# Normalisation ahead of the rotation in a softmax pipeline, and an interleaved tail behind the last experts

## The chip, the cores and the metric

The kernel runs on one core of a Trainium2 chip. The metric is the device time in microseconds of one execution, as the median of several runs. All matrices and activations are float32. Where a matmul must be accurate, the kernel splits an operand into a high part (`_hi`, type fp32r) and the rest (`_lo`), and adds the products; a full f32 matmul is used for the smaller products and appears in the trace as two records.

## What is computed

The kernel computes a two-layer block (retention, RWKV, gated units, FFN; untouched here), and then a second block with dilated attention, memory cross-attention and a mixture of experts, closed by a root-mean-square norm. Cut to what the change touches:

```python
def rms_norm(t, g):
    tf = t.astype(jnp.float32)
    y = tf * lax.rsqrt(jnp.mean(tf * tf, axis=-1, keepdims=True) + NORM_EPS)
    return (y * g.astype(jnp.float32)).astype(t.dtype)

# dilated attention, 12 heads of 64 channels, 512 tokens
qf, kf = rotary_2(q, positions), rotary_2(k, positions)
s = einsum(qf, kf) * HEAD_DIM ** -0.5        # masked
m = jnp.max(s, axis=-1)
p = jnp.exp(s - m[..., None]); den = jnp.sum(p, axis=-1)
o = einsum(p, v) / den

# second block, its end
h = rms_norm(x, moe_norm_g)
x = x + hierarchical_moe(h, ...)             # 32 experts, top 2 of a group
return rms_norm(x, final_norm_g)
```

## The kernel before

Activations lie transposed in SBUF: `xT` is 128 partitions by 8 tiles by 512 tokens. Each engine has its own instruction list, written out by hand in the order in which it runs; engines meet at semaphores only (`wait_ge`, `then_inc`). There is no scheduler, so the order in the source is the order of execution.

**The middle stage** (`mid_phase`) is a row of 62 jobs `n`, each one weight tile times activations on TensorE, into PSUM bank `n % 2`. For each job ScalarE makes the high part of the weights (`high`, a cast) and GpSimd the low part (`low`, a subtraction of two SBUF tiles, 128x1024), one or two jobs ahead. Between the jobs lies the attention. It handles the heads in six pairs `g`, each spread over four steps that go with jobs `n = 8 + 4g` to `11 + 4g` (`att_step(n)` gives `g, step`). Its parts are:

- `turn` (TensorE) and `half_turn`, `times_cos`, `finish_turn` (VectorE, GpSimd, VectorE): the rotation of q and k. It follows one job behind the jobs listed in `TURNED` (4, 5, 8, 9, 10, 11, 14 to 17, 20, 21). `half_turn` frees the rotation's PSUM bank, and `finish_turn` needs the product by GpSimd.
- `scores(g, s)` (TensorE), `mask_scores(g, s)` (VectorE: adds the band and takes the row maximum), `exps(g, s)` (ScalarE), all with `s` = the step, in steps 0 and 1. `s` says which half of the query tiles.
- `normalise(g, s)` (VectorE): a reciprocal of the sums and four divisions of 128x512, in step `s + 1`. It waits for the exponentials of half `s`.
- `swing(g, u)` (TensorE): 16 transposes of the probabilities of head `u`, in steps 2 and 3. In step 2 it waits for six divisions of the pair, that is, for two of the four in `normalise(g, 1)`. `take_swung` copies the result out of PSUM on VectorE and ScalarE; `values` multiplies by v.
- `tap`: the depthwise convolution, four multiply-adds per step on VectorE until job 20. `take_mem_k` (jobs 22 to 29) and `put` (pairs 3 to 5) are further work of VectorE in the same steps.

**The expert stage** (`experts_phase`) handles 32 experts, two at a time (`g` = 0 to 15), in quads. Per two experts TensorE multiplies up (L3098), turns the result (L3122) and multiplies down in two halves of 512 columns (`y_banks`, L3133). ScalarE writes `y_hi` and VectorE `y_lo` of each half (L3210, L3278). `scatter(g, k)` (L3110, L3111) brings tile `k` of the result back to the tokens, in one of the two `add_banks`, and `add` (L3231) adds the bank to `xT`. For all but the last two experts the scatters lie between the matmuls of the next up product.

**The end.** Behind the last experts' block the flag `again` is loaded (L3315) to see whether an expert had more than 64 tokens; the body under the `If` holds further rounds. Then `norm_phase` squares the eight tiles on ScalarE (L180), sums them over the partitions on TensorE by a matmul with ones (L194), takes the root by Ln and Exp (L134, L136) and scales on VectorE into `hT` (L206). A last block sends `hT` out as one DMA (L3358) and waits for it. Between two blocks all engines meet.

## Time and profile before

| | |
|---|---|
| median of 3 runs | 3269.89 us (3269.32 to 3277.79) |
| the profiled execution | 3263.98 us, of it span 3262.1 us |
| granted TensorE clock, mean | 0.963 of full |
| TensorE matmul busy | 2996.3 us, 92% |
| VectorE busy | 1239.5 us, 38% |
| ScalarE busy | 1039.2 us, 32% |
| GpSimd busy | 1056.6 us, 32% |

The attention stretch of the middle stage lies at 2250 to 2480 us, the expert stage at 2750 to 3233 us. Everything is told against the span of the one profiled execution; the median of the runs is 5.9 us above that execution's own time. In a timeline, a row merges instructions of a kind that follow each other; the bracket at its end is the idle time of that engine just before, and what ended it. Where a row of matmuls is longer than its like, the granted clock was lower. PEld is TensorE's weight load, SPq the queue of the engine that issues DMAs.

### The profile page before, as it was taken

To read this page: it belongs to the slowest core of one execution; us is meant where nothing else is said; L and a number is where in the kernel's file an instruction comes from. 1 tells how busy PE (TensorE), PEld (TensorE's weight loads), DVE (VectorE), ACT (ScalarE), POOL (GpSimd) and SP (SyncE) were. 2 spreads that over 40 slices of the span, in tenths; PEclk is the share of its full clock that TensorE was granted. 3 is DMA by queue.
4 is the path that set the end of the run, shared out by engine and by line. 5 is a ranking of instruction groups with operands and counts; after the bars stand their busy time and mean duration, and the time that the engine had idled before them with its cause. 6 is when DMAs were issued, how large, how long until landed. Compare 5 with 4: busy or idle time off the path is not lost. (4 is left out here: it accounts for less than half of the span.)

```text
span 3262.1 us, 48752 instructions
## 1 busy us (share of the span) xinstructions
PE 2996.3 (92%) x20676; PEld 2256.8 (69%) x20677; DVE 1239.5 (38%) x1762; ACT 1039.2 (32%) x1525; POOL 1056.6 (32%) x635
## 2 busy tenths in 40 slices
PE   5997989989999699798999999989888998999997
PEld 4776878878888577597887888857666764444542
DVE  2248424334440124842333444037764323222222
ACT  3443233333332235322423333235345331111111
POOL 2343224434444233422443444423334330011000
PEclk8998999999999899899999999989999999999998
DMA  3220022212222222001222222221112236999994
GB/s 129 69 72 26 4 82 91 90 66 95 99 105 89 89 78 71 31 4 63 97 91 79 79 102 100 89 93 52 52 54 93 66 141 261 374 401 401 399 378 181
DMA packets 52911, 402.71 MB, mean 123 GB/s; under 512 B 7008, under 2 KB 8160, under 8 KB 12512
## 3 DMA queue, kind: packets, MB, share of 16 engines
q1 hardware_dynamic: 52704, 399.72, 32.2%
q8 instruction: 157, 2.57, 0.3%
q14 instruction: 50, 0.41, 0.0%
HBM read 397.60 MB, written 2.10 MB: 123 GB/s over the span
## 5 line engine op out<-in xcount | busy, mean ns | idle before, releaser
L1138 POOL TENSOR_TENSOR back_w_lo<-w,back_w_hi 128x1024 fp32r<-128x1024 f32 (+1 forms) x248 | 537.4, 2177 | 751.1 <-ACT back_w_hi L1347 751.0
L1347 ACT CAST back_w_hi<-w 128x1024 fp32r<-128x1024 f32 (+1 forms) x248 | 236.8, 955 | 809.9 <-PE bank L1166 773.6
L1161 PE MATMUL bank<-h_hi,back_w_hi 128*128 128x512 f32 x1056 | 265.9, 394 | 11.1 <-ACT back_w_hi L1347 11.1
L1163 PE MATMUL bank<-h_lo,back_w_hi 128*128 128x512 f32 x1056 | 260.8, 389 | 0.0
L1166 PE MATMUL bank<-h_hi,back_w_lo 128*128 128x512 f32 x1056 | 260.8, 389 | 0.0
L322 POOL TENSOR_TENSOR front_w_lo<-w,front_w_hi 128x1024 fp32r<-128x1024 f32 x68 | 167.6, 2467 | 245.8 <-ACT front_w_hi L499 245.8
L1161 PEld LDWEIGHTS bank<-h_hi,back_w_hi 128*128 128x128 f32 x1056 | 200.1, 190 | 56.4 <-ACT back_w_hi L1347 13.1
L3098 PE MATMUL bank<-moe_w,moe_hg 128*64 128x512 f32 x1024 | 232.5, 597 | 0.0
L1897 POOL TENSOR_TENSOR mid_w_lo<-w,mid_w_hi 128x1024 fp32r<-128x1024 f32 x62 | 150.4, 2427 | 246.9 <-ACT mid_w_hi L2357 246.6
L1163 PEld LDWEIGHTS bank<-h_lo,back_w_hi 128*128 128x128 f32 x1056 | 198.3, 188 | 41.3
L1166 PEld LDWEIGHTS bank<-h_hi,back_w_lo 128*128 128x128 f32 x1056 | 198.2, 188 | 41.1
L3098 PEld LDWEIGHTS bank<-moe_w,moe_hg 128*64 128x64 f32 x1024 | 71.0, 137 | 134.9 <-issue 134.9
L1544 DVE SCALAR_TENSOR_TENSOR back_conv<-bank,back_taps,back_conv 128x511 f32<-128x511 f32 x88 | 66.0, 750 | 255.2 <-ACT back_conv L1448 255.2
L377 PE MATMUL bank<-h_hi,front_w_hi 128*128 128x512 f32 x416 | 119.9, 433 | 44.9 <-ACT front_w_hi L499 44.9
L499 ACT CAST front_w_hi<-w 128x1024 fp32r<-128x1024 f32 x68 | 70.9, 1046 | 255.9 <-PE bank L382 200.9
L3231 DVE TENSOR_TENSOR xT<-xT,bank 128x512 f32<-128x512 f32 x128 | 82.3, 683 | 170.2 <-PE bank L3111 170.2
L1511 DVE TENSOR_TENSOR xT<-xT,bank 128x512 f32<-128x512 f32 (+1 forms) x36 | 22.6, 628 | 307.0 <-PE bank L1166 305.2
L377 PEld LDWEIGHTS bank<-h_hi,front_w_hi 128*128 128x128 f32 x416 | 80.6, 199 | 77.4 <-issue 60.5
L3133 PE MATMUL bank<-moe_w,moe_midT 128*64 128x512 f32 x512 | 113.4, 595 | 12.1 <-ACT moe_midT L3205 12.1
L382 PE MATMUL bank<-h_hi,front_w_lo 128*128 128x512 f32 x416 | 109.0, 405 | 12.4 <-POOL front_w_lo L322 12.4
L3039 POOL COPY moe_quad_place<-moe_place 128x16 f32 (+1 forms) x7 | 1.4, 198 | 365.7 <-PE bank L3117 365.7
L2357 ACT CAST mid_w_hi<-w 128x1024 fp32r<-128x1024 f32 x62 | 64.8, 1045 | 159.4 <-PE bank L1976 97.3
(544 smaller groups left out, 5690.6 us busy)
## 6 DMA issues: line engine op xcount, KB each, us to landing
moe_w<-in_moe_w SPq DMA_DIRECT2D x128, 1024.0 KB, 11.5
moe_w<-in_moe_w SPq DMA_DIRECT2D x32, 2048.0 KB, 11.7
w<-in_ffn_up SPq DMA_DIRECT2D x44, 1024.0 KB, 4.8
w<-in_w_merge SPq DMA_DIRECT2D x24, 1536.0 KB, 6.4
w<-in_w_in SPq DMA_DIRECT2D x34, 1024.0 KB, 4.8
w<-in_w_mid SPq DMA_DIRECT2D x31, 1024.0 KB, 4.8
w<-in_ffn_down SPq DMA_DIRECT2D x16, 1408.0 KB, 6.0
w<-in_w_out SPq DMA_DIRECT2D x16, 512.0 KB, 4.1
```

The costliest lines, as they stand in the source:

```text
L322: nc.gpsimd.tensor_tensor(split(w_lo, c, t), raw(c, t), split(w_hi, c, t).bitcast(F32), ALU.subtract).then_inc(f["w_lo"], 1)
L377: nc.tensor.matmul(T.ps[t][:, :], w_hi[:, t, k, :], h_hi[:, k, :], start=(k == 0), stop=False)
L382: mm = nc.tensor.matmul(T.ps[t][:, :], w_lo[:, t, k, :], h_hi[:, k, :], start=False, stop=(k == KD - 1))
L1138: nc.gpsimd.tensor_tensor(split(B.w_lo, n), raw(n), split(B.w_hi, n).bitcast(F32), ALU.subtract).then_inc(f["w_lo"], 1)
L1161: nc.tensor.matmul(bank, B.w_hi[:, n % 2, k, :], x_hi[:, cols], start=start and k == 0, stop=False)
L1163: nc.tensor.matmul(bank, B.w_hi[:, n % 2, k, :], x_lo[:, cols], start=False, stop=False)
L1166: mm = nc.tensor.matmul(bank, B.w_lo[:, n % 2, k, :], x_hi[:, cols], start=False, stop=stop and k == len(hi) - 1)
L1347: nc.scalar.copy(split(B.w_hi, n), raw(n)).then_inc(f["w_hi"], 1)
L1897: nc.gpsimd.tensor_tensor(split(B.w_lo, n), raw(n), split(B.w_hi, n).bitcast(F32), ALU.subtract).then_inc(f["w_lo"], 1)
L3098: mm = nc.tensor.matmul(bank[half_of(u), :], hg[:, k, slots_of(b, u)], w[:, u, k * 512:k * 512 + 512], start=(k == 0), stop=(k == KD - 1))
L3133: mm = nc.tensor.matmul(y_banks[half][half_of(u), :], midT[:, f, half_of(u)], w2[:, u, c:c + 512], start=(f == 0), stop=(f == 3))
L3231: nc.vector.tensor_tensor(T.xT[:, k, :], T.xT[:, k, :], add_banks[k % 2][:, :], ALU.add).then_inc(sems["added"], 1)
```

## The change

1. In `mid_phase`, VectorE's `normalise` moves ahead of `half_turn`, `mask_scores` and `finish_turn` of the same step. 
2. For the last two experts the scatters use six PSUM banks in turn (6, 7, 4, 5, 0, 1) instead of two. The first four start when `y_lo`'s first half is there. VectorE adds tiles 0 and 1 before it makes the second half of `y_lo`. 
3. The squares of the final norm are taken on ScalarE tile by tile behind the adds, in four buffers, and summed on TensorE between the last scatters; ScalarE runs an Ln on one column first. The root is taken inside the expert block.
4. `norm_phase` and the last block give way to `out_phase`: eight scalings on VectorE, each followed by its own DMA of 256 KB, the clearing of the semaphores behind them, and one wait for all.

On VectorE, in step 2 of pair 0 (job 10), the list was, from the end of the masks of step 1. L2660 is `finish_turn`, L2680 and L2684 are `normalise`, L2736 `tap`, L2652 `half_turn`, L2691 `take_swung`:

```order
L2674 TENSOR_SCALAR mid_st_10211<-mid_st_10211 128x2x2
L2660 TENSOR_TENSOR mid_qk_10167<-mid_qk_10167,mid_rot_tmp_10171 128x512
L2680 RECIPROCAL mid_st_10211<-mid_st_10211 128x2x2
L2684 TENSOR_SCALAR mid_sc_10179<-mid_sc_10179,mid_st_10211 128x512 x4
L2736 SCALAR_TENSOR_TENSOR mid_ag_10185<-mid_padded_10187,mid_par_10189,mid_ag_10185 128x512 x4
L2652 TENSOR_TENSOR mid_rot_tmp_10171<-bank,mid_table_10169 128x512
L2660 TENSOR_TENSOR mid_qk_10167<-mid_qk_10167,mid_rot_tmp_10171 128x512
L2680 RECIPROCAL mid_st_10211<-mid_st_10211 128x2x2
L2684 TENSOR_SCALAR mid_sc_10179<-mid_sc_10179,mid_st_10211 128x512 x4
L2691 COPY mid_pT_10181<-bank 128x512 x2
```

and is now (the same names, one line further down):

```order
L2675 TENSOR_SCALAR mid_st_10215<-mid_st_10215 128x2x2
L2661 TENSOR_TENSOR mid_qk_10171<-mid_qk_10171,mid_rot_tmp_10175 128x512
L2737 SCALAR_TENSOR_TENSOR mid_ag_10189<-mid_padded_10191,mid_par_10193,mid_ag_10189 128x512 x4
L2681 RECIPROCAL mid_st_10215<-mid_st_10215 128x2x2
L2685 TENSOR_SCALAR mid_sc_10183<-mid_sc_10183,mid_st_10215 128x512 x4
L2653 TENSOR_TENSOR mid_rot_tmp_10175<-bank,mid_table_10173 128x512
L2661 TENSOR_TENSOR mid_qk_10171<-mid_qk_10171,mid_rot_tmp_10175 128x512
L2692 COPY mid_pT_10185<-bank 128x512 x2
```

The first `normalise` has left this piece, upwards past the masks; the second stands ahead of the two rotation operations instead of behind them.

On VectorE, in step 1 of pair 4 (job 25), where nothing is rotated; L2697 is `put`, L2775 `take_mem_k`, L2669 the first of four masks:

```order
L2674 TENSOR_SCALAR mid_st_10211<-mid_st_10211 128x2x2
L2697 SCALAR_TENSOR_TENSOR h_lo<-bank,gains,h_hi_10060 128x512
L2775 TENSOR_TENSOR mid_mem_k_10191<-bank,mid_r_10200_10201 128x256
L2669 ISA mid_sc_10179,mid_st_10211<-bank,mid_band_10177 128x512
L2669 ISA mid_st_10211 128x1
```

and now:

```order
L2698 SCALAR_TENSOR_TENSOR h_lo<-bank,gains,h_hi_10060 128x512
L2776 TENSOR_TENSOR mid_mem_k_10195<-bank,mid_r_10204_10205 128x256
L2681 RECIPROCAL mid_st_10215<-mid_st_10215 128x2x2
L2685 TENSOR_SCALAR mid_sc_10183<-mid_sc_10183,mid_st_10215 128x512 x4
L2670 ISA mid_sc_10183,mid_st_10215<-bank,mid_band_10181 128x512
L2670 ISA mid_st_10215 128x1
```

The reciprocal and the four divisions now stand between `take_mem_k` and the masks; they stood behind the masks.

On TensorE, at the end of the program, from the last scatter (L3110, L3111) over the flag and the blocks to the sums (L194):

```order
L3110 MATMUL bank<-moe_selT_10149,moe_y_hi_10159 128x512
L3111 MATMUL bank<-moe_selT_10149,moe_y_lo_10161 128x512
L2990 UNCONDITIONAL_BRANCH
L3319 UNCONDITIONAL_BRANCH
L3319 REGISTER_ALU
L3319 COMPARE_AND_BRANCH
L3317 REGISTER_ALU
L3317 COMPARE_AND_BRANCH
L167 UNCONDITIONAL_BRANCH
L189 UNCONDITIONAL_BRANCH
L194 MATMUL bank<-sq,ones 128x512 x8
```

and now, with scatters at L3121 and L3122 and sums at L3128:

```order
L3121 MATMUL bank<-moe_selT_10153,moe_y_hi_10163 128x512
L3122 MATMUL bank<-moe_selT_10153,moe_y_lo_10165 128x512
L3128 MATMUL bank<-moe_out_sq_10083,ones 128x512
L3121 MATMUL bank<-moe_selT_10153,moe_y_hi_10163 128x512
L3122 MATMUL bank<-moe_selT_10153,moe_y_lo_10165 128x512
L3128 MATMUL bank<-moe_out_sq_10083,ones 128x512 x5
L2991 UNCONDITIONAL_BRANCH
```

The sums moved ahead of the end of the block: three lie between scatters, five behind the last.

The diff:

```diff
@@ -1775,6 +1775,7 @@
         self.h_hi, self.h_lo = at(80, "h_hi", 4, D, dt=F32R), at(96, "h_lo", 4, D, dt=F32R)
         self.xg, self.sq, self.sq_sum = at(112, "xg", 2, S), at(116, "sq", 2, S), at(120, "sq_sum", S)
         self.lgT, self.r_row = at(122, "lgT", S), at(124, "r_row", S)
+        self.out_sq, self.out_root = at(112, "out_sq", 4, S), at(120, "out_root", S)
 
         top[0] = T.w_home + KD * 1024
         self.wr, self.bias, self.iota = then("wr", KD, G + E), then("bias", G + E), then("iota", E)
@@ -2911,15 +2912,15 @@
                     dve.wait_ge(f["done"], n + 1)
                     nc.vector.tensor_tensor(xT[:, n - CROSS_OUT, :], xT[:, n - CROSS_OUT, :], T.ps[n % 2][:, :],
                                             ALU.add).then_inc(f["took"][n % 2], 1)
+                g, step = att_step(n)
+                if step in (1, 2):
+                    normalise(g, step - 1)
                 if n - 1 in TURNED:
                     half_turn(n - 1)
-                g, step = att_step(n)
                 if step in (0, 1):
                     mask_scores(g, step)
                 if n - 1 in TURNED:
                     finish_turn(n - 1)
-                if step in (1, 2):
-                    normalise(g, step - 1)
                 if step in (2, 3):
                     take_swung(g, step - 2)
                 if summed_pair(n) is not None and summed_pair(n) >= 3:
@@ -2960,7 +2961,7 @@
 
 MOE_SEMS = ("up_full*2 w2_full staged sel_ready gates_ready gates_summed gates_taken selT_done selT_taken gathered "
             "hg_act hg_dve up_half up_done silu_done made mid_turned midT_taken down_done y_hi y_lo scattered added "
-            "clock maxed exped gates_made")
+            "clock maxed exped gates_made x_squared x_summed out_rooted")
 
 
 def fetch_up(sync, T, sems, M, n):
@@ -2989,6 +2990,7 @@
     place, gate, slot_gate = M.quad_place, M.quad_gate, M.slot_gate
     with nc.Block() as block:
         up_banks, y_banks, hg_banks, add_banks = T.ps[0:2], T.ps[2:4], T.ps[4:6], T.ps[6:8]
+        last_banks = [T.ps[b] for b in (6, 7, 4, 5, 0, 1)]
 
         def half_of(u):
             return slice(SLOTS * u, SLOTS * u + SLOTS)
@@ -3110,6 +3112,35 @@
                 nc.tensor.matmul(add_banks[k % 2][:, :], y_hi[:, k * P:k * P + P], selT[:, :], start=True, stop=False)
                 nc.tensor.matmul(add_banks[k % 2][:, :], y_lo[:, k * P:k * P + P], selT[:, :], start=False,
                                  stop=True).then_inc(sems["scattered"], 1)
+
+            def scatter_last(g, k):
+
+                if k >= len(last_banks):
+                    pe.wait_ge(sems["added"], KD * g + k - len(last_banks) + 3)
+                bank = last_banks[k % len(last_banks)]
+                nc.tensor.matmul(bank[:, :], y_hi[:, k * P:k * P + P], selT[:, :], start=True, stop=False)
+                nc.tensor.matmul(bank[:, :], y_lo[:, k * P:k * P + P], selT[:, :], start=False,
+                                 stop=True).then_inc(sems["scattered"], 1)
+
+            def sum_last(k):
+
+                pe.wait_ge(sems["x_squared"], k + 1)
+                nc.tensor.matmul(y_banks[0][:, :], T.ones[:, :], M.out_sq[:, k % 4, :], start=(k == 0),
+                                 stop=(k == KD - 1)).then_inc(sems["x_summed"], 1)
+
+            def scatter_and_sum(g):
+
+                pe.wait_ge(sems["added"], KD * g + 2)
+                pe.wait_ge(sems["gates_taken"], quads)
+                pe.wait_ge(sems["y_lo"], 2 * g + 1)
+                for k in range(4):
+                    scatter_last(g, k)
+                pe.wait_ge(sems["y_lo"], 2 * g + 2)
+                for k in range(4, KD):
+                    scatter_last(g, k)
+                    sum_last(k - 4)
+                for k in range(4, KD):
+                    sum_last(k)
 
             def turn_and_down(g, s, b):
 
@@ -3161,11 +3192,10 @@
                         pe.wait_ge(sems["hg_act"], 2 * q + 2 * b + 3)
                         pe.wait_ge(sems["hg_dve"], 2 * q + 2 * b + 3)
                         up(g + 1, 1 - b, step)
+                        scatter(g, 6)
+                        scatter(g, 7)
                     else:
-                        for k in (2, 4, 6):
-                            step(k)
-                    scatter(g, 6)
-                    scatter(g, 7)
+                        scatter_and_sum(g)
 
         @block.scalar
         def _(act):
@@ -3213,6 +3243,16 @@
                         silu(g + 1, s, 1)
                     elif more:
                         silu(g + 1, 1 - s, 0)
+                    else:
+                        nc.scalar.activation(M.scratch[:, :], T.ones[:, 0:1], ACT.Ln)
+                        for k in range(KD):
+                            act.wait_ge(sems["added"], KD * g + k + 3)
+                            if k >= 4:
+                                act.wait_ge(sems["x_summed"], k - 3)
+                            nc.scalar.activation(M.out_sq[:, k % 4, :], T.xT[:, k, :], ACT.Square).then_inc(
+                                sems["x_squared"], 1)
+                        act.wait_ge(sems["x_summed"], KD)
+                        rsqrt(act, sems["out_rooted"], 0, M.out_root[:, :], y_banks[0][:, :], 1.0 / D, T.eps(EPS))
 
         @block.vector
         def _(dve):
@@ -3225,6 +3265,11 @@
                 nc.vector.scalar_tensor_tensor(out=mid[:, :], in0=up_banks[1][:, :],
                                                scalar=slot_gate[:, s, 2 * b + 1:2 * b + 2], in1=sil[:, :],
                                                op0=ALU.mult, op1=ALU.mult).then_inc(sems["made"], 1)
+
+            def add_last(g, k):
+                dve.wait_ge(sems["scattered"], KD * g + k + 1)
+                nc.vector.tensor_tensor(T.xT[:, k, :], T.xT[:, k, :], last_banks[k % len(last_banks)][:, :],
+                                        ALU.add).then_inc(sems["added"], 1)
 
             def add(g, k):
                 dve.wait_ge(sems["scattered"], KD * g + k + 1)
@@ -3272,20 +3317,28 @@
                     if b == 1 and more:
                         rows(q + 1, 1)
                         rows(q + 1, 3)
+                    final = b == 1 and not more
                     for half in range(2):
+                        if final and half == 1:
+                            for k in range(2):
+                                add_last(g, k)
                         o = slice(512 * half, 512 * half + 512)
                         dve.wait_ge(sems["y_hi"], 2 * g + half + 1)
                         nc.vector.scalar_tensor_tensor(out=y_lo[:, o], in0=y_banks[half][:, :],
                                                        scalar=slot_gate[:, s, 2 * b:2 * b + 1], in1=y_hi[:, o].bitcast(F32),
                                                        op0=ALU.mult, op1=ALU.subtract).then_inc(sems["y_lo"], 1)
-                    for k in range(6):
-                        add(g, k)
-                    if b == 0:
-                        gated(g + 1, s, 1)
-                    elif more:
-                        gated(g + 1, 1 - s, 0)
-                    add(g, 6)
-                    add(g, 7)
+                    if final:
+                        for k in range(2, KD):
+                            add_last(g, k)
+                    else:
+                        for k in range(6):
+                            add(g, k)
+                        if b == 0:
+                            gated(g + 1, s, 1)
+                        else:
+                            gated(g + 1, 1 - s, 0)
+                        add(g, 6)
+                        add(g, 7)
 
 
 def next_places_phase(nc, stale, M):
@@ -3300,8 +3353,27 @@
             nc.vector.tensor_scalar(M.place[:, :, :], M.place[:, :, :], float(-SLOTS), None, ALU.add)
 
 
-def block_two(nc, T):
-    sems, xT, hT = T.sems, T.xT, T.hT
+def out_phase(nc, T, sems, stale, gain, root, out):
+
+    with nc.Block() as block:
+        @block.vector
+        def _(dve):
+            for k in range(KD):
+                nc.vector.scalar_tensor_tensor(out=T.hT[:, k, :], in0=T.xT[:, k, :], scalar=gain[:, k:k + 1],
+                                               in1=root[:, :], op0=ALU.mult, op1=ALU.mult).then_inc(sems["scaled"], 1)
+
+        @block.sync
+        def _(sync):
+            for k in range(KD):
+                sync.wait_ge(sems["scaled"], k + 1)
+                sync.dma_start(out[:, k, :], T.hT[:, k, :]).then_inc(T.sems["stored"]["done"], 16)
+            clear(sync, stale)
+            sync.wait_ge(T.sems["stored"]["done"], 16 * KD)
+            clear(sync, sems)
+
+
+def block_two(nc, T, out):
+    sems = T.sems
     norm2, head = sems["norm2"], sems["head"]
     gain = lambda name: T.g2[:, GCOLS[name][0]:GCOLS[name][1]]
     with ExitStack() as ctx:
@@ -3325,7 +3397,7 @@
                             @block.sync
                             def _(sync):
                                 clear(sync, moe)
-    norm_phase(nc, T, norm2, moe, xT, gain("final_norm_g_2"), hT)
+        out_phase(nc, T, norm2, moe, gain("final_norm_g_2"), M.out_root, out)
 
 
 
@@ -3350,14 +3422,7 @@
                 nc.gpsimd.memset(T.ones[:, :], 1.0)
 
         block_one(nc, T)
-        block_two(nc, T)
-        with nc.Block() as block:
-            @block.sync
-            def _(sync):
-                clear(sync, T.sems["norm2"])
-                sync.dma_start(out, T.hT[:, :, :]).then_inc(T.sems["stored"]["done"], 16)
-
-                sync.wait_ge(T.sems["stored"]["done"], 16)
+        block_two(nc, T, out)
```

## Rows read from the trace of the kernel before

**Rows 1.** Waits 2240 to 2480: waiter, releaser, us in total, times, longest.

```profile
PE bank L2082 <- DVE mid_sc L2684: 29.2, 6, 8.3
```

**Rows 2.** TensorE timeline, attention stretch: start us, us, operation, idle before.

```profile
2261.57 2.11 PE L1961 MATMUL bank<-h_hi,mid_w_hi 128*128 128x512 f32 x8
...
2267.15 1.02 PE L2054 MATMUL bank<-mid_qk,mid_rot 128*128 128x512 f32 x2
2273.74 3.65 PE L2082 MATMUL bank<-ident,mid_sc 128*128 128x128 f32 x16 [5.57 <-DVE mid_sc L2684]
2277.03 2.92 PE L1961 MATMUL bank<-h_hi,mid_w_hi 128*128 128x512 f32 x8
...
2284.28 1.91 PE L2082 MATMUL bank<-ident,mid_sc 128*128 128x128 f32 x16
...
2315.80 3.11 PE L2082 MATMUL bank<-ident,mid_sc 128*128 128x128 f32 x16 [3.93 <-DVE mid_sc L2684]
...
2360.03 3.65 PE L2082 MATMUL bank<-ident,mid_sc 128*128 128x128 f32 x16 [5.41 <-DVE mid_sc L2684]
...
2403.48 3.65 PE L2082 MATMUL bank<-ident,mid_sc 128*128 128x128 f32 x16 [8.30 <-DVE mid_sc L2684]
...
2435.28 3.12 PE L2082 MATMUL bank<-ident,mid_sc 128*128 128x128 f32 x16 [3.03 <-DVE mid_sc L2684]
```

**Rows 3.** VectorE timeline, the same stretch.

```profile
2259.76 0.69 DVE L2652 TENSOR_TENSOR mid_rot_tmp<-bank,mid_table 128x512 f32<-128x512 f32 x1 [1.87 <-PE bank L2054]
...
2264.30 1.67 DVE L2684 TENSOR_SCALAR mid_sc<-mid_sc,mid_st 128x512 f32<-128x512 f32 x4
2265.89 2.73 DVE L2736 SCALAR_TENSOR_TENSOR mid_ag<-mid_padded,mid_par,mid_ag 128x512 f32<-128x512 f32 x4
...
2269.85 2.74 DVE L2660 TENSOR_TENSOR mid_qk<-mid_qk,mid_rot_tmp 128x512 f32<-128x512 f32 x1 [0.63 <-POOL mid_qk L1915]
...
2312.64 3.80 DVE L2684 TENSOR_SCALAR mid_sc<-mid_sc,mid_st 128x512 f32<-128x512 f32 x4
...
2352.06 2.73 DVE L2736 SCALAR_TENSOR_TENSOR mid_ag<-mid_padded,mid_par,mid_ag 128x512 f32<-128x512 f32 x4
...
2426.66 0.69 DVE L2669 CUSTOM_DVE_ANT_0 mid_sc<-bank,mid_band 128x512 f32<-128x512 f32 x1 [0.57 <-PE bank L2068]
...
2429.23 1.81 DVE L2674 TENSOR_SCALAR mid_st<-mid_st 128x4 f32<-128x4 f32 x1
```

**Rows 4.** ScalarE timeline, the same stretch.

```profile
2265.74 0.71 ACT L2414 ACTIVATE mid_sc<-mid_sc,mid_st 128x512 f32<-128x512 f32 x1
...
2310.25 0.71 ACT L2414 ACTIVATE mid_sc<-mid_sc,mid_st 128x512 f32<-128x512 f32 x1
...
2396.06 1.03 ACT L2357 CAST mid_w_hi<-w 128x1024 fp32r<-128x1024 f32 x1
```

**Rows 5.** GpSimd timeline, the same stretch.

```profile
2426.30 4.71 POOL L1897 TENSOR_TENSOR mid_w_lo<-w,mid_w_hi 128x1024 fp32r<-128x1024 f32 x2
```

**Rows 6.** Timeline of the last 40 us, all engines.

```profile
3225.74 0.50 PE L3110 MATMUL bank<-moe_selT,moe_y_hi 128*128 128x512 f32 x1 [1.57 <-DVE moe_y_lo L3278]
...
3226.51 1.28 DVE L3231 TENSOR_TENSOR xT<-xT,bank 128x512 f32<-128x512 f32 x2 [0.83 <-PE bank L3111]
...
3232.63 0.69 DVE L3231 TENSOR_TENSOR xT<-xT,bank 128x512 f32<-128x512 f32 x1 [0.19 <-PE bank L3111]
3234.31 4.26 ACT L180 ACTIVATE sq<-xT 128x512 f32<-128x512 f32 x8 [9.41 <-PEq L2990]
...
3237.74 8.93 PE L194 MATMUL bank<-sq,ones 128*128 128x512 f32 x16 [5.15 <-ACT sq L180]
...
3249.37 5.39 DVE L206 SCALAR_TENSOR_TENSOR hT<-xT,gains,rstd 128x512 f32<-128x512 f32 x8 [16.05 <-ACT rstd L136]
```

**Rows 7.** DMA issues of the whole run: KB each, us from issue to landing.

```profile
out<-hT SPq DMA_DIRECT2D x1, 2048.0 KB, 6.3
...
front_up<-in_rw_up SPq DMA_DIRECT2D x2, 256.0 KB, 2.7
```

## The prediction

> **What bounds the kernel now.** I read the list of waits over the attention stretch first, since the reordering lies there. TensorE's one large wait is for the second half of the softmax divisions: 29.2 us in six waits, one for each pair of heads [rows 1]. TensorE's timeline shows each one [rows 2]: idle 5.57 us before the transposes at 2273.74, then 3.93, 5.41, 8.30 and 3.03 for pairs 1 to 4, which leaves 3.0 of the 29.2 for pair 5. The granted clock costs more behind them: the 16 transposes take 3.65 us after the first wait and 1.91 us where TensorE came from work (2284.28), and the eight matmuls behind take 2.92 instead of 2.11 us [rows 2]. That is 1.74 + 0.8 = 2.5 us beyond the wait. TensorE is the engine all others follow here, so what it stops waiting for comes off the end. The tail is a chain with no cover: the last adds of x, squares, sums, root, scaling, one 2 MB output DMA [rows 6, 7].
>
> **Part 1: normalise ahead of the rotation.** VectorE's order inside a step changes, the work does not. I name the four steps of a pair 0 to 3; mask_scores runs in steps 0 and 1, normalise in 1 and 2, TensorE's transposes (swing) in 2 and 3. Swing of step 2 needs six divisions: two of step 2's four.
>
> Pair 0, before: the last exponential of step 1 ends at 2265.74 + 0.71 = 2266.45 [rows 4]. VectorE did step 1's divisions (2264.30, 1.67 us) and then the taps (2265.89 to 2268.6), then half_turn, then finish_turn, 2.74 us long from 2269.85 instead of 0.69 because GpSimd was in it, then the divisions [rows 3]. TensorE had finished its turn matmul at 2267.15 + 1.0 = 2268.1 [rows 2]. After: step 1's divisions need step 0's exponentials, which are done by then; they fall into the 1.87 us in which VectorE sat idle before half_turn at 2259.76 [rows 3], so taps start 1.8 us earlier and end at about 2266.8. A reciprocal (0.2) and two divisions (0.4 each) end at 2267.8, ahead of TensorE's 2268.1. The wait of 5.57 goes and so does the slow clock: 5.6 + 2.5 = **8.1 us**. What is late next is finish_turn, still stretched by GpSimd, and the copies behind it (end near 2274); TensorE asks for those only after its next job, near 2276.5, so 2 us of cover stay.
>
> Pair 1 has no rotation in its step 2. Its divisions ran at 2312.64 for 3.80 us, one of the four held up by GpSimd [rows 3]. With step 1's divisions moved into idle time the taps end 1.9 us earlier, and the exponentials, which end at 2310.25 + 0.71 = 2311.0 [rows 4], become the last thing. Two divisions after them end at 2312.1, TensorE is ready at 2315.80 - 3.93 = 2311.9. Gain 3.6 us of wait, and 3.11 - 1.91 = 1.2 of clock: **4.8 us**. Pair 2 is like pair 0: its taps, 2352.06 to 2354.8 [rows 3], end 1.9 earlier, two divisions and a reciprocal end at 2353.9, TensorE is ready at 2360.03 - 5.41 = 2354.6. Gain 5.4 + 1.7 + about 0.4 = **7.5 us**. Pair 3: TensorE's job in front is short, so it is ready at 2403.48 - 8.30 = 2395.2, but the exponentials end only at 2396.1, where ScalarE starts its next cast [rows 4]. Two divisions would end at 2397.5; if GpSimd's next subtraction gets in first, at 2399.9. A wait of 2.3 to 4.7 us stays, and with it part of the slow clock. Gain 3.6 to 8; I take **6.4 us**, as the next GpSimd operation needs that cast, 1.03 us long.
>
> Pairs 4 and 5 are where the order hurts. They rotate nothing and their step 2 is unchanged; in step 1 the four divisions now stand in front of mask_scores. There VectorE has no idle time: after taking mem_k it waits 0.57 us for the scores, and the masks start at 2426.66 [rows 3]. Unhindered, 1.9 us of divisions would delay the masks by 1.3 us, and this would be free, because the small operation behind the masks (2429.23, 1.81 us for 4 columns) is waiting for GpSimd anyway until 2431.0 [rows 3, 5]. But GpSimd runs two subtractions without a gap from 2426.30 for 4.71 us [rows 5], and a division is held up by one, as pair 1's row shows (3.80 against 1.67 for four) [rows 3]. So one division gets in ahead, one between the two, two after 2431.3; the masks begin near 2432.5 instead of 2426.66. From there, masks 2.6, exponentials 3.0, reciprocal and two divisions 1.0: TensorE starts at 2439.2 instead of 2435.28 [rows 2]. That **costs 3.9 us**, and pair 5 has the same pattern and the same price. Queued behind the blocked divisions are the masks, behind these ScalarE's exponentials and TensorE's swing. Ends: 0 (the divisions slip through) and 5 us each.
> The Trainium skill, page "SBUF — State Buffer", section "SBUF: two separate sides", says that VectorE and GpSimd share a port pair under an exclusive lock held for a whole instruction, and the loser waits fully. The rows agree with it; without the rule as a lock (as shared bandwidth) this term would be near 1 us for each pair.
> Sum of part 1: 8.1 + 4.8 + 7.5 + 6.4 - 3.9 - 3.9 = **19.0 us**, ends 9 and 29.
>
> **Part 2: the tail.** TensorE is free at 3225.74 - 1.57 = 3224.17 and the first half of y_lo exists, so four scatters can start there instead of at 3225.74 [rows 6]. A scatter reaches its add in 3226.51 - 3225.74 = 0.77 us, so the first add starts at 3224.95, about where the second half of y_lo starts now; the two adds put in front take 1.28 [rows 6], so that y_lo and the scatters that need it come at 3225.74 + 1.28 = 3227.0. From 3227.0 TensorE runs four scatters (0.5 each, two matmuls of one pass) and eight sums. A sum is one f32 matmul of 512 columns, recorded as two; the turn matmul of this kind takes 1.02 with its drain [rows 2], so 0.9 in a row. 2.0 + 7.2: the sums end at **3236.2** instead of 3237.74 + 8.93 = 3246.7 [rows 6]. Adds (0.64) and squares (0.53, eight in 4.26) are shorter than 1.4 us for each tile, and ScalarE's table load for Ln falls while VectorE is still adding, so all hide under TensorE; if they did not, the old 8.93 would not shrink. The root keeps its second table load: 3246.7 to 3249.37, 2.7 us, to 3238.9. New in the path is the end of the block with the load of the "again" flag, which formerly stood between the last add (3233.32) and the squares (3234.31): 1.0 us, now after the root: 3239.9. Scaling 5.39: 3245.3. The output now leaves in eight DMAs of 256 KB, one per 0.67 us; only the last is exposed: 2.7 us, as the 256 KB load landed, instead of 6.3 [rows 7], and the clearing of some 37 semaphores hides behind it. Before, 3262.1 - 3254.8 = 7.3 us lay behind the scaling, 6.3 of it the DMA; now 1.0 + 2.7, so the end is 3249.0. Gain **13.1 us**.
> Ends: if all sums ran at half the clock, 7 us less; if the eight DMAs queue up (eight times 1.0 us is more than 5.4), 2.5 us less; 14.5 at best. So 4 to 14.5. I take the upper part, since TensorE's gap is 0.9 us where the clock fell before after gaps of 1.57 and more.
>
> **Sum.** 19.0 + 13.1 = 32.1 us off a span of 3262.1: 3230.0, and 3231.9 for this execution, which took 3263.98. The median of the runs is 3269.89, so **3237.8 us**. The 5.9 us between that execution and the median are spread that I can't place; the range takes it in.
>
> **Rivals.**
> A. Forecast: 20 to 37 us gained. 0.62.
> B. The divisions of pairs 4 and 5 get through, or the delay hides under the 1.81 us stall: both terms vanish: 40 us, 3230. For: the stall is there already. Against: GpSimd's 4.71 us in one piece. 0.17.
> C. Only the tail pays: the waits of pairs 0 to 3 move from the first swing to the second (its copies queue behind a finish_turn of 2.7 us) or to the rotated pair: 11 to 16 us, 3256. For: VectorE's own chain is long, GpSimd stretches it. Against: 2 us of cover in pair 0, counted above. 0.12.
> D. Slower. The four divisions block the masks in step 1 of all six pairs as they do in two: 6 x 3.9 = 23.4 lost, the exponentials come as much later so no wait shrinks, and the tail gives 13.1 back: 10 us more, 3280. It decides where the scores of step 1 land before the divisions are done. The tightest of pairs 0 to 3 is pair 0, with 1.87 us idle against 1.9 us of divisions: half_turn would move by 0.3 us only, so this needs GpSimd in those gaps too. 0.04.
> E. It does not do what it says: TensorE's half clock in the sums, queued DMAs and blocked divisions leave under 10 us. 3265. 0.05.
> A difference under 0.3%, 9.8 us, can't be told from none in this kernel. Faster: A + B + C = 0.91; same 0.05; slower 0.04. The range takes A and B whole and C's better half: 3223 (40 us off, and the lower level of the profiled execution) to 3256.
>
> **What would show it.** Right: TensorE's wait for the divisions at 12 us or less in all instead of 29.2, with the waits of pairs 0 to 2 gone and transposes of 1.9 us; those of pairs 4 and 5 at 7 us each, with divisions of over 2 us in front of the masks. Sums ending 11.5 to 12.5 us after the last down matmul (before 22.5); last output DMA landing under 3 us after its issue. Wrong: waits of pairs 0 to 3 reappearing at other lines, pairs 4 and 5 unchanged (B), or the sums' matmuls at twice their length.

## The result, and the profile after

| | before | changed |
|---|---|---|
| median of 4 runs each | 3271.08 us (3269.32 to 3277.79) | 3236.61 us (3230.46 to 3240.0) |
| ratio of the times, 95% interval | | 0.9889 [0.9866, 0.9911] |
| the profiled execution | 3263.98 us, span 3262.1 us | 3233.63 us, span 3231.8 us |
| TensorE matmul busy | 2996.3 us | 2988.6 us |

The forecast was 3237.8 us. The span fell by 30.3 us. Three marks cut it up: the issue of the `mid_band` DMA, which stands ahead of the attention; the issue of the router weights' DMA behind it; and the end of the last down matmul.

| stretch | before | changed | gain |
|---|---|---|---|
| start to `mid_band` | 2168.6 | 2169.4 | -0.8 |
| `mid_band` to router weights (attention) | 337.0 | 316.2 | 20.8 |
| router weights to the last down matmul | 718.6 | 720.3 | -1.7 |
| last down matmul to the end of the span | 37.9 | 25.9 | 12.0 |

The first and third stretch hold nothing that was changed; their part is run-to-run spread (see the third group of experiments). So the two parts of the change are worth 20.8 and 12.0 us.

The waits of the attention stretch of the changed kernel, with waiter, releaser, us in total, times, longest; before there were 29.2 us in six [rows 1]:

```profile
PE bank L2083 <- DVE mid_sc L2685: 16.2, 4, 6.8
```

TensorE's timeline, changed kernel (start us, us, operation, idle before). These are the swings of pairs 0 to 5; of pair 0 the second one is shown too:

```profile
2268.66 1.94 PE L2083 MATMUL bank<-ident,mid_sc 128*128 128x128 f32 x16
...
2276.76 1.91 PE L2083 MATMUL bank<-ident,mid_sc 128*128 128x128 f32 x16
...
2304.81 1.94 PE L2083 MATMUL bank<-ident,mid_sc 128*128 128x128 f32 x16 [0.46 <-DVE mid_sc L2685]
...
2341.79 1.91 PE L2083 MATMUL bank<-ident,mid_sc 128*128 128x128 f32 x16
...
2377.17 2.38 PE L2083 MATMUL bank<-ident,mid_sc 128*128 128x128 f32 x16 [2.24 <-DVE mid_sc L2685]
...
2411.85 3.64 PE L2083 MATMUL bank<-ident,mid_sc 128*128 128x128 f32 x16 [6.75 <-DVE mid_sc L2685]
...
2445.26 3.65 PE L2083 MATMUL bank<-ident,mid_sc 128*128 128x128 f32 x16 [6.74 <-DVE mid_sc L2685]
```

Pairs 0 and 2 wait no more, and where TensorE comes from work the transposes take 1.91 to 1.94 us instead of 3.65 [rows 2]. Pairs 4 and 5 wait 6.7 us instead of 3.0. On VectorE the reason for both stands in a few rows:

```profile
2259.07 1.67 DVE L2685 TENSOR_SCALAR mid_sc<-mid_sc,mid_st 128x512 f32<-128x512 f32 x4
...
2264.77 2.73 DVE L2737 SCALAR_TENSOR_TENSOR mid_ag<-mid_padded,mid_par,mid_ag 128x512 f32<-128x512 f32 x4
...
2267.63 1.67 DVE L2685 TENSOR_SCALAR mid_sc<-mid_sc,mid_st 128x512 f32<-128x512 f32 x4
...
2270.55 2.79 DVE L2661 TENSOR_TENSOR mid_qk<-mid_qk,mid_rot_tmp 128x512 f32<-128x512 f32 x1 [0.65 <-POOL mid_qk L1916]
...
2399.06 5.91 DVE L2685 TENSOR_SCALAR mid_sc<-mid_sc,mid_st 128x512 f32<-128x512 f32 x4
2404.89 0.68 DVE L2670 CUSTOM_DVE_ANT_0 mid_sc<-bank,mid_band 128x512 f32<-128x512 f32 x1
```

In pair 0 the first four divisions fill the idle time at 2259, the taps start at 2264.77 instead of 2265.89 [rows 3], and the second four run at 2267.63 in 1.67 us. `finish_turn`, still held up by GpSimd (2.79 us), now comes behind them. In pair 4 the four divisions ahead of the masks take 5.91 us. GpSimd at the same time as these last:

```profile
2399.16 5.13 POOL L1898 TENSOR_TENSOR mid_w_lo<-w,mid_w_hi 128x1024 fp32r<-128x1024 f32 x2
```

The cost depends on idle time as well. In step 1 of pairs 2 and 3 GpSimd holds up the same four divisions (4.84 us from 2328.38, 4.89 us from 2364.11). In the kernel before VectorE sat idle there for 5.01 and 5.58 us, and it still waits 0.38 us for the scores of TensorE ahead of its next masks, as it did, so nothing is late.

The tail of the changed kernel, all engines; it answers to [rows 6]. L3121 is a scatter, L3271 an add of the last experts, L3252 the squares, L3128 the sums, L3362 the scaling, L3369 the output's DMAs:

```profile
3205.83 0.50 PE L3121 MATMUL bank<-moe_selT,moe_y_hi 128*128 128x512 f32 x1
...
3206.60 1.28 DVE L3271 TENSOR_TENSOR xT<-xT,bank 128x512 f32<-128x512 f32 x2 [2.61 <-PE bank L3122]
3206.65 1.28 ACT L3247 ACT_TABLE_LOAD   x1
...
3208.60 0.50 PE L3121 MATMUL bank<-moe_selT,moe_y_hi 128*128 128x512 f32 x1 [0.65 <-DVE moe_y_lo L3327]
...
3213.14 4.45 PE L3128 MATMUL bank<-moe_out_sq,ones 128*128 128x512 f32 x10
...
3217.63 0.69 ACT L134 ACTIVATE moe_out_root<-bank,scalars 128x512 f32<-128x512 f32 x1 [2.75 <-PE bank L3128]
3218.34 1.28 ACT L136 ACT_TABLE_LOAD   x1
3219.63 0.63 ACT L136 ACTIVATE moe_out_root<-moe_out_root 128x512 f32<-128x512 f32 x1
3221.36 5.39 DVE L3362 SCALAR_TENSOR_TENSOR hT<-xT,gains,moe_out_root 128x512 f32<-128x512 f32 x8 [7.33 <-PEq L2991]
3222.14 6.06 SPq L3369 DMA_DIRECT2D out<-hT  x8
```

The last down matmul ends at 3205.90 by the trace's modelled end, and the first scatter follows at once; before it came 1.57 us behind. The sums end at 3213.14 + 4.45 = 3217.59, 11.7 us behind that matmul, where they took 3246.7 - 3224.2 = 22.5. Their last ten records take 0.445 us each; in the row of before, behind 5.15 us of idle time, they took 8.93 / 16 = 0.56 [rows 6]. The granted clock accounts for this: it was 0.50 of full from 3237.7 to 3241.0 and 1.00 from 3243.0 in the kernel before, and 1.00 over all the sums in the changed one.

### The profile page after: what moved, and what is told of

Its sections match the earlier page's. It is cut to its first block and busy times, and to the rows that moved or that the text cites. A ratio compares the mean times of both kernels' runs of the same rounds, so it can differ in the third digit from the quotient of the medians.

```text
span 3231.8 us, 48755 instructions
## 1 busy us (share of the span) xinstructions
PE 2988.6 (92%) x20676; PEld 2251.3 (70%) x20677; DVE 1244.0 (38%) x1762; ACT 1039.7 (32%) x1526; POOL 1057.2 (33%) x635
## 3 DMA queue, kind: packets, MB, share of 16 engines
q8 instruction: 157, 2.57, 0.3%
## 5 line engine op out<-in xcount | busy, mean ns | idle before, releaser
L1161 PEld LDWEIGHTS bank<-h_hi,back_w_hi 128*128 128x128 f32 x1056 | 200.1, 190 | 56.3 <-ACT back_w_hi L1347 13.1
```

The costliest lines, as they stand in the source:

```text
L1161: nc.tensor.matmul(bank, B.w_hi[:, n % 2, k, :], x_hi[:, cols], start=start and k == 0, stop=False)
```

## The experiments

**How they are read.** For each pair I take the time from the first score matmul of pair 0 (2251.22 before, 2251.82 changed) to the second swing of the pair. What lies ahead of it cancels out, and the number repeats to 0.1 us as a rule, and 0.4 us at the most, in kernels that have the same order up to there. Four kernels ran only once (each half of the divisions alone, the short subtractions, the single output DMA); of these only times between places in the profile are compared, not the whole time.

### The two parts, each alone

The kernel before with the divisions moved, and nothing else:

```diff
+                g, step = att_step(n)
+                if step in (1, 2):
+                    normalise(g, step - 1)
                 if n - 1 in TURNED:
                     half_turn(n - 1)
-                g, step = att_step(n)
                 if step in (0, 1):
                     mask_scores(g, step)
                 if n - 1 in TURNED:
                     finish_turn(n - 1)
-                if step in (1, 2):
-                    normalise(g, step - 1)
```

> Part 1 alone: the divisions ahead of the rotation, the tail as before. My theory: 20 us off the kernel before, made of 8 + 5 + 7.5 + 7 us for pairs 0 to 3 and two losses of 4 us at pairs 4 and 5; TensorE's waits for the divisions about 0, 0.5, 0, 2.2, 6.7 and 6.7 us. The ratio to before would be 0.994. Rival: the gain of the whole change comes from the tail and from the level of a run, and the stretch only moves its waits elsewhere: then under 10 us.

Measured: 3251.46 us, ratio 0.994 [0.9921, 0.9958], and an attention stretch of 316.2 us, as in the changed kernel. The waits are 0, 0.46, 0, 2.24, 6.75 and 6.75 us.

The other half is the changed kernel with that edit taken back:

> Part 2 alone: the attention stretch as before, the tail of the change. My theory: 12 us off, the span behind the last down matmul 26 us instead of 37.9, ratio 0.996; the six waits for the divisions come back with 29 us. Rival: parts 1 and 2 help each other, so that each alone gives clearly less than its share and the two add up to less than 28 us.

Measured: 3256.76 us, ratio 0.9957 [0.9944, 0.997], stretch 336.9 us, waits of 29.3 us, and 25.7 us behind the last down matmul. The two parts touch different ends of the program, and their gains add up: 0.6% and 0.43% against 1.11%, and between the marks each alone gives what it gives in the changed kernel. Both rivals are out: the stretch does gain by itself, and neither part needs the other.

### Which half of the divisions does it

`normalise` moved in both steps. I moved it in one at a time. The changed kernel with only step 1's divisions ahead (for step 2's alone, the two conditions change places):

```diff
-                if step in (1, 2):
+                if step == 1:
                     normalise(g, step - 1)
...
                 if n - 1 in TURNED:
                     finish_turn(n - 1)
+                if step == 2:
+                    normalise(g, step - 1)
```

> Only the divisions of the first half (step 1) stand ahead of rotation and masks; those of step 2 stay behind finish_turn, as before. Theory: where a rotation lies in step 2 (pairs 0, 2, 3) it is the rotation that keeps TensorE waiting, so pairs 0 and 2 keep their waits (over 4.5 us each) and gain 0 to 1 us; pair 3 gains about 3, pair 1, which rotates nothing in step 2, gains its whole 5; pairs 4 and 5 lose 4 and 3.5 as in the changed kernel. The attention stretch (issue of mid_band's DMA to issue of the router weights' DMA, 337.0 us before, 316.2 changed) comes to 335 to 336. Rival: the taps alone were in the way, which now end 1.9 us earlier everywhere: pairs 0 and 2 gain most of their 8, and the stretch comes to 320.

> Only the divisions of the second half (step 2) stand ahead of the rotation; those of step 1 stay behind the masks. Theory: the taps of step 1 end 1.9 us later than in the changed kernel, so waits of about 1.6 us (pair 0) and 1.3 us (pair 2) stay, gains 5.5 and 6; pair 1 has the same order in step 2 as before and gains 0; pair 3 gains 1.5, as its taps end at 2400; pairs 4 and 5 neither gain nor lose. In all 13: the stretch comes to 324. With the half tried beside it the gains would come to about 15 of the 20.8 us, so the halves help each other. Rival: the gains simply add up, and this one has 337.0 + 316.2 minus the other's stretch.

Measured, as the gain of each pair over the kernel before (us, by the reading above):

| pair | changed | step 1 alone | step 2 alone |
|---|---|---|---|
| 0 | 8.1 | 0.3 | 0.7 |
| 1 | 5.2 | 5.2 | 0.1 |
| 2 | 7.6 | -0.7 | 0.4 |
| 3 | 6.9 | 2.8 | 1.9 |
| 4 | -4.1 | -4.0 | 0.0 |
| 5 | -3.4 | -3.9 | -0.1 |
| sum | 20.2 | -0.4 | 3.0 |

With step 1 alone the pairs come out as the theory said, the waits of pairs 0 and 2 staying at 5.41 and 5.40 us. The stretch was 340.4 us, over the 335 to 336 forecast: the pairs came to -0.4 where I had expected +1.5, and 3 us more lie ahead of the first score matmul and behind the last swing, where nothing differs. Its rival (the taps alone were in the way) is out.

With step 2 alone I was wrong by 10 us (13 expected, 3.0 measured; the stretch shows no gain at all, 337.2 us, since here too 3 us more lie ahead of the first score matmul and behind the last swing). I had priced the taps' lateness of 1.9 us as lateness and nothing more. TensorE waited 4.49 us in pair 0 and 4.32 in pair 2, not 1.6 and 1.3. VectorE of that kernel in pair 0, then GpSimd:

```profile
2272.88 2.73 DVE L2737 SCALAR_TENSOR_TENSOR mid_ag<-mid_padded,mid_par,mid_ag 128x512 f32<-128x512 f32 x4
...
2275.74 4.55 DVE L2685 TENSOR_SCALAR mid_sc<-mid_sc,mid_st 128x512 f32<-128x512 f32 x4
```

```profile
2275.31 1.43 POOL L1916 TENSOR_TENSOR mid_qk<-mid_qk,mid_table 128x512 f32<-128x512 f32 x1 [4.82 <-PE bank L2055]
2276.70 2.52 POOL L1898 TENSOR_TENSOR mid_w_lo<-w,mid_w_hi 128x1024 fp32r<-128x1024 f32 x1
```

The divisions start 0.43 us behind GpSimd's product for the rotation and are caught by it and by the subtraction behind it: 4.55 instead of 1.67 us. TensorE needs two of them; the second ends at 2279.50, and its transposes start at 2279.64. GpSimd's product in the changed kernel:

```profile
2268.91 1.53 POOL L1916 TENSOR_TENSOR mid_qk<-mid_qk,mid_table 128x512 f32<-128x512 f32 x1 [4.68 <-PE bank L2055]
```

There the divisions start at 2267.63, 1.28 us ahead of it, and the fourth at 2268.82, 0.09 us ahead of it; all four run undisturbed. So the half moved in step 1 is what brings step 2's divisions ahead of GpSimd, and the half moved in step 2 is what lets them use it. Alone they give -0.4 and 3.0 us, together 20.2. The rival for this run, that the gains add up, falls too: its own sum would have given 337.0 + 316.2 - 340.4 = 312.8 us of stretch, and 337.2 were measured.

### Pairs 4 and 5: GpSimd's lock, or the place

First the divisions of step 1 of these two pairs back behind the masks:

```diff
-                if step in (1, 2):
+                if step == 2 or step == 1 and g < 4:
                     normalise(g, step - 1)
...
                     finish_turn(n - 1)
+                if step == 1 and g >= 4:
+                    normalise(g, step - 1)
```

> The changed kernel, but in step 1 of pairs 4 and 5 the divisions stand behind the masks again. My theory: the change pays at pairs 0 to 3 and costs 3.5 to 4 us each at pairs 4 and 5, where VectorE has no idle time ahead of the masks; the waits there return from 6.7 to 3.0 us, and the kernel is 7.5 us faster than the changed one, 40 us below the kernel before (ratio 0.988). Rival: pairs 4 and 5 wait longer because everything ahead of them runs earlier and something of fixed time (weights, casts) is now late; then the waits stay at 6.7 us.

Measured: waits of 3.04 and 3.02 us, so the rival (everything merely runs earlier there) is out. From the first score matmul to the last swing the kernel is 7.4 us shorter than the changed one, where 7.5 had been expected; the stretch, 309.6 us, is 6.6 us shorter, since 0.8 come back behind the last swing. The medians, 3236.43 against 3236.61 us, and the ratio to before, 0.9891 where 0.988 had been expected, did not show it; the next group takes that up.

Next, the places as in the changed kernel, but with short operations on GpSimd:

```diff
                 pool.wait_ge(f["w_hi"], n + 1)
-                nc.gpsimd.tensor_tensor(split(B.w_lo, n), raw(n), split(B.w_hi, n).bitcast(F32),
-                                        ALU.subtract).then_inc(f["w_lo"], 1)
+                cut = slice(0, 1) if n in (26, 27, 30, 31) else slice(None)
+                nc.gpsimd.tensor_tensor(split(B.w_lo, n)[:, cut, :], raw(n)[:, cut, :],
+                                        split(B.w_hi, n).bitcast(F32)[:, cut, :], ALU.subtract).then_inc(f["w_lo"], 1)
```

> The changed kernel, in which GpSimd makes only an eighth of the low parts of the weights of jobs 26, 27, 30 and 31 (part of the computation is left out): 128x128 instead of 128x1024 elements, four operations of about 0.3 instead of 2.35 us. Theory (GpSimd's long operations hold the divisions up): the four divisions ahead of the masks of pairs 4 and 5 take under 2.4 us instead of 5.9, the masks start about 1.3 us late instead of 4.9, TensorE's waits there fall from 6.7 to 3 us or less, and the attention stretch from 316.2 to 308 to 310. Rival (the place of the divisions alone costs it): waits stay over 5 us.

Measured: waits of 2.92 and 3.45 us instead of 6.75 and 6.74, stretch 308.6 us. VectorE in pairs 4 and 5, then GpSimd in pair 4, whose row ends with both short operations:

```profile
2401.76 2.08 DVE L2686 TENSOR_SCALAR mid_sc<-mid_sc,mid_st 128x512 f32<-128x512 f32 x4
2403.76 0.68 DVE L2671 CUSTOM_DVE_ANT_0 mid_sc<-bank,mid_band 128x512 f32<-128x512 f32 x1
...
2430.92 2.61 DVE L2686 TENSOR_SCALAR mid_sc<-mid_sc,mid_st 128x512 f32<-128x512 f32 x4
```

```profile
2400.49 1.28 POOL L1922 TENSOR_TENSOR mid_a_sum<-mid_a_sum,mid_sq 128x512 f32<-128x512 f32 x1 [10.74 <-ACT mid_sq L2436]
2401.86 1.30 POOL L1899 TENSOR_TENSOR mid_w_lo<-w,mid_w_hi 128x128 fp32r<-128x128 f32 x2
```

With the place unchanged and only GpSimd's operations short, the divisions fall from 5.91 and 5.90 to 2.08 and 2.61 us, and the waits to about what they are with the divisions behind the masks (3.04 and 3.02). It is the length of GpSimd's operations, not the place by itself. In pair 5 the two limits that I had set, 2.4 us for the divisions and 3 us for the wait, were missed: the weights of jobs 30 and 31 lie in another shape, the edit left a quarter of their low parts (128x256) and not an eighth, and the two operations came to 1.84 us, not 0.6.

The Trainium skill, "SBUF — State Buffer", section "SBUF: two separate sides", calls the shared ports an exclusive lock held for the whole instruction. That agrees with the 5.91 us: two operations of GpSimd, 5.13 us with what slips in between, lie inside them.

Last, GpSimd's subtraction deferred behind the divisions of these two pairs, on top of the first edit of this group:

```diff
             def low(n):
+                if n in (27, 31):
+                    pool.wait_ge(f["normed"], 2 * (n - 27) + 40)
                 pool.wait_ge(f["w_hi"], n + 1)
```

> As the last one, and GpSimd makes the low parts of the weights of jobs 27 and 31 only when all eight divisions of pair 4 or 5 are done. My theory: the 1.8 us in which VectorE's small operation behind the masks waits for GpSimd goes away, the exponentials start that much earlier, TensorE's waits at pairs 4 and 5 fall from 3.0 to about 1.4 us, with some of the slow clock behind them; 3 to 5 us in all beyond the last one. Rival: the low parts come too late for TensorE and the wait reappears in jobs 27 and 31: no gain or a loss.

Measured: 3226.45 us, ratio 0.9856 [0.9839, 0.9873], waits of 1.68 and 1.40 us. From the first score matmul to the last swing it is 4.9 us shorter than the kernel without the deferral (2.9 in pair 4, 2.0 in pair 5), within the 3 to 5 expected. The stretch, 307.5 us, shows only 2.1 of them: 1.7 us more lie ahead of the first score matmul, where nothing differs, and 1.1 come back behind the last swing. The same pair of kernels in the next group has stretches of 309.6 and 306.0 us. The rival is out: TensorE waited for a low part once in the stretch, for 0.3 us. Pair 5 gains less than pair 4 for a reason that the rows show. TensorE, VectorE and GpSimd behind pair 4 of this kernel, in order of time:

```profile
2413.78 1.94 PE L2085 MATMUL bank<-ident,mid_sc 128*128 128x128 f32 x16 [1.68 <-DVE mid_sc L2687]
...
2414.50 2.39 POOL L1900 TENSOR_TENSOR mid_w_lo<-w,mid_w_hi 128x1024 fp32r<-128x1024 f32 x1 [5.99 <-DVE mid_sc L2687]
...
2417.17 5.06 POOL L1900 TENSOR_TENSOR mid_w_lo<-w,mid_w_hi 128x1024 fp32r<-128x1024 f32 x2 [0.28 <-ACT mid_w_hi L2360]
...
2417.47 2.51 DVE L2759 TENSOR_SCALAR mid_ag<-mid_ag,mid_par 128x512 f32<-128x512 f32 x1
...
2419.90 2.88 DVE L2756 SCALAR_TENSOR_TENSOR mid_ag<-mid_ag,mid_par,mid_padded 128x512 f32<-128x512 f32 x1
...
2424.98 1.99 PE L2071 MATMUL bank<-mid_qk 64*128 64x512 f32 x8 [1.77 <-DVE mid_pT L2694]
```

The deferred subtraction and the two behind it now meet VectorE's next work on SBUF tiles, whose single operations take 2.51 and 2.88 us (undisturbed ones take 0.5 to 0.7); the copies of the transposes queue behind it, and the next scores wait 1.77 us for them, a wait that the kernel without the deferral doesn't have. A part of what the deferral took off one step fell on the next.

### Do the gains of the stretch reach the end?

Three of the kernels again, with six, six and four runs, all on the same chip.

> The changed kernel again, beside the next two on the same chip. Attention stretch 316.2 us, profiled span about 3232, ratio to the kernel before 0.989.

> Pairs 4 and 5 with their first half behind the masks, a second time in more rounds. Theory: stretch 309.6 us, 6.6 us off the changed kernel's, ratio 0.987. Rival: the gain is given back in the expert stage, as the medians so far (3236.43 and 3236.61 us) say; ratio 0.989 and a span as the changed kernel's.

> The same with GpSimd's two subtractions deferred behind the divisions, in more rounds: stretch 307.5 us, 2 us off the one ahead, ratio 0.986; the best of the three if the gains of the stretch reach the end.

| kernel | median us | ratio to before, 95% | stretch | rest before the tail | behind last down |
|---|---|---|---|---|---|
| changed | 3240.56 | 0.991 [0.9894, 0.9927] | 320.2 | 724.4 | 25.6 |
| pairs 4 and 5 back | 3228.97 | 0.9886 [0.987, 0.9903] | 309.6 | 718.8 | 25.6 |
| and subtraction deferred | 3224.55 | 0.9864 [0.9845, 0.9883] | 306.0 | 718.8 | 26.3 |

The order is the one that the stretches gave: the last beats the changed kernel by 16 us in the medians here and by 10 in the earlier runs, somewhat more than the 8.7 us of the stretch (316.2 against 307.5), and the intervals here do not touch. For the last kernel the rival, that the gain is given back, is out. For the middle one it is less clear: its interval overlaps both others, and its ratio, 0.9886, lies nearer to the rival's 0.989 than to the theory's 0.987. What speaks against the rival is that five of its six runs are below the fastest of the changed kernel (3234.38 us) and that nothing between the stretch and the end is longer in its profile. Two expectations for the changed kernel itself were missed: a stretch of 320.2 us instead of 316.2, and a span of 3244.3 instead of about 3232.

The spread shows itself beside this. In this profile of the changed kernel the second swings of all six pairs lie within 0.4 us of those of the first, and yet its span is 3244.3 instead of 3231.8 us: 4.6 us ahead of `mid_band`, 4.1 in the stretch (3.7 of them ahead of the first score matmul and behind the last swing), 4.1 between the router weights and the last down matmul. Windows around the start of the expert stage, first of this profile, then of the first one, at about the same place of the program (from, to, length, busy us of TensorE, its weight load, VectorE, ScalarE and GpSimd, then granted clock, DMA share, GB/s):

```profile
2720.00:2790.00 70.00, 66.06 (x344) 29.91 (x342) 13.50 (x20) 8.89 (x14) 7.12 (x19) 0.95 0.91 371
```

```profile
2711.60:2781.60 70.00, 66.05 (x358) 30.45 (x355) 14.41 (x22) 8.89 (x14) 7.12 (x19) 1.00 0.95 388
```

TensorE is as busy, with a granted clock of 0.95 instead of 1.00, and 344 matmul records instead of 358. Such stretches come and go between executions of one kernel. What decides when they come I don't know; no run tests it.

### The output: eight DMAs or one

```diff
-            for k in range(KD):
-                sync.wait_ge(sems["scaled"], k + 1)
-                sync.dma_start(out[:, k, :], T.hT[:, k, :]).then_inc(T.sems["stored"]["done"], 16)
+            sync.wait_ge(sems["scaled"], KD)
+            sync.dma_start(out, T.hT[:, :, :]).then_inc(T.sems["stored"]["done"], 16)
             clear(sync, stale)
-            sync.wait_ge(T.sems["stored"]["done"], 16 * KD)
+            sync.wait_ge(T.sems["stored"]["done"], 16)
```

> The changed kernel with its output in one DMA of 2 MB behind the last scaling, as before, instead of eight of 256 KB. From the end of the scaling to the end of the span: 5.05 us in the changed kernel. Theory: with one DMA it takes the 6.3 us that the DMA took before, and about 1 us around it, 7.3 us: 2.3 us later. Rival: eight small DMAs move their data more slowly (2 KB packets at under 400 GB/s against 477) and gain less than that, or nothing: 5 to 6 us with one DMA as well.

Measured: the scaling ends at 3227.2, the span at 3234.2, so 7.0 us instead of 5.05. That is close to the theory's 7.3 and rules the other out. Eight DMAs save 1.95 us by these two profiles, where my prediction had 3.6. Over the ten profiles with eight DMAs this stretch is 4.73 to 5.45 us long, over the three with one DMA 7.0 to 7.4, so the saving is known to 1.5 to 2.7 us only. The DMA rows of the whole run, changed kernel and this one (KB each, median us from issue to landing):

```profile
out<-hT SPq DMA_DIRECT2D x8, 256.0 KB, 3.1
```

```profile
out<-hT SPq DMA_DIRECT2D x1, 2048.0 KB, 6.3
```

And the tail of the changed kernel in windows, the scaling ending at 3226.75 (columns as above):

```profile
3224.00:3226.00 2.00, 0.00 (x0) 0.00 (x0) 2.00 (x4) 0.00 (x0) 0.00 (x0) 0.50 0.95 349
3226.00:3228.00 2.00, 0.00 (x0) 0.00 (x0) 0.74 (x2) 0.00 (x0) 0.00 (x0) 0.50 1.02 375
3228.00:3230.00 2.00, 0.00 (x0) 0.00 (x0) 0.00 (x0) 0.00 (x0) 0.00 (x0) 0.50 0.52 196
```

From 3224 to 3228 the DMA engines are full, at 349 and 375 GB/s; the single DMA moved its data at 393 GB/s from 3229 to 3233, so the rival's premise, that the small ones are slower, holds in part, and only its conclusion does not. At 375 GB/s, 2 MB take 5.6 us (an estimate from this rate), as long as the scaling itself (5.39), so the transfers fall behind it: the first lands 2.7 us behind its issue, the last 4.3 us.

## Why the prediction was right, point by point

The forecast (case A, 3237.8 us) came within 1.2 us of the median. Against the profiled execution, where the sum was made, it was 32.1 us of gain against 30.3; the changed parts gave 32.8, and 2.5 were lost to spread in stretches that nothing touched. That the median agreed so closely is in part luck: part 1 gave 1.8 us more than forecast and part 2 1.1 less, and the changed kernel itself gave 3236.61 and 3240.56 us on two occasions.

| term | predicted us | measured us |
|---|---|---|
| pair 0 | 8.1 | 8.1 |
| pair 1 | 4.8 | 5.2 |
| pair 2 | 7.5 | 7.6 |
| pair 3 | 6.4 | 6.9 |
| pairs 4, 5 | -3.9, -3.9 | -4.1, -3.4 |
| part 1 | 19.0 | 20.2 (stretch 20.8) |
| part 2 | 13.1 | 12.0 |

- **Pairs 0 and 2.** In pair 0 as worked out: taps end at 2267.50 (2266.8 forecast, with the 0.6 us by which this run is later there), two divisions by 2268.5, TensorE comes from its turn matmul at 2268.66. The slow clock went with the wait. The margin over TensorE was 0.2 us. Pair 2's wait is gone as well, and its gain is 7.6 us. What the prediction did not see is the second margin, that to GpSimd's product 1.28 us behind the start of the divisions; the step 2 run showed that 1.9 us later, which I had priced at 1.6 us of wait, costs 4.5.
- **Pair 1.** A wait of 0.46 us stayed where I had about 0.2; transposes back at 1.94 us.
- **Pair 3.** I took a wait of 2.3 to 4.7 us. It was 2.24, just under the lower end, and a quarter of the slow clock's price stayed (2.38 us for the transposes, between 1.91 and 3.65). GpSimd's subtraction did catch the divisions (2376.14, 3.80 us for four), but only behind the two that TensorE needs.
- **Pairs 4 and 5.** The mechanism was as told, one division ahead, one between, two behind; the masks of pair 4 started at 2404.89, and TensorE waited 6.75 instead of 3.03 us. The short operations on GpSimd showed it. So rival B, by which these divisions get through, did not come. Nor did C: the waits of pairs 0 to 3 did not reappear at other lines (over the whole stretch TensorE's waits at other lines come to 7.7 us, before to 9.1), and the stretch is shorter by what they lost. Nor D: in pairs 0 to 3 the four divisions of step 1 fell into idle time, even in pairs 2 and 3, where GpSimd stretched them to 4.84 and 4.89 us. The lower end that I gave part 1, 9 us, is not the sum of its terms: with 3.6 us for pair 3 and 5 lost in each of pairs 4 and 5 it would be 14.
- **Tail.** Sums 11.7 us behind the last down matmul (12.0 forecast), root 2.67 (2.7), from the root to the scaling 1.1 (1.0), scaling 5.39. The one term that was mis-sized is the last: 5.05 us instead of 1.0 + 2.7 = 3.7. I took the landing of a DMA of 256 KB standing alone for the last of eight, which took 4.3 us; the queueing that I named as a bound (2.5 us) cost 1.35 in all. TensorE's clock did not fall in the sums, as assumed: it was 1.00 of full.
- **The signs that I named.** The divisions ahead of the masks, the vanished waits of pairs 0 and 2, the transposes of 1.9 us in pairs 0 to 2 (0.46 us of wait stayed in pair 1) and the sums at 11.7 us came as told. Two signs failed. TensorE's waits for the divisions came to 16.2 us in all, not to 12 or less; my own terms, 7 us each for pairs 4 and 5 and 2.3 for pair 3, already added up to 16.3. And the last output DMA landed 4.3 us behind its issue, not under 3.
- **What I left unplaced.** The 5.9 us between the profiled execution and the median stay unplaced, as the execution that gave the median has no profile. Untouched parts of the program do spread by that much over these thirteen profiles: the part ahead of `mid_band` ends between 2168.6 and 2174.6 us, and the rest before the tail takes 718.6 to 724.4 us. Longer executions also have the lower mean clock (0.958 at 3278.84 us against 0.963 at 3266.22, both of the kernel before).

## What to carry to other kernels

When an operation is moved, compare its new start with what the other engine on the shared ports runs there: 1.9 us of lateness cost 4.5 us of wait in one place, and four short divisions took 5.9 us in another. A move can help in some iterations of a loop and hurt in others, so look at each one; making it conditional on the pair took 6.6 us more off the stretch. An operation that is held up costs only where its engine has no idle time to take it: 4.9 us of divisions cost nothing in pair 3 and 5.9 us cost four in pair 4. Small gains are read between two marks inside the program that enclose the edit closely, since the whole time here spreads by more than they are worth, and so did even the stretch, by 4.1 us between two profiles of one kernel.
